# A hybrid decoder step on one core: four value pages per TensorE round, causal pooling as banded products, page suffix sums under the input GEMM

## The chip, the cores and the metric

The kernel runs on one core of a Trainium2 chip. The metric is the device time of one execution in microseconds (us). The profile shows the five engines: TensorE (PE, with PEld for its weight loads), VectorE (DVE), ScalarE (ACT), GpSimd (POOL) and SyncE (SP), whose queue issues most DMA transfers.

## The reference, cut to what matters

The program is one step of a two-layer decoder, for a prompt of 1024 tokens and for 8 decode samples with 2048 past positions each. All of it is computed; the change touches only the mixer of layer 0, which has two parts.

```
# A) forgetting attention, 8 heads x 64
logf = log_sigmoid(fl + b_forget)
# prompt: sc = q.k * scale + c_i - c_j, causal softmax, p @ v
# sample: keys and values gathered by page_table, 16 pages of 128 positions
lf_all = concatenate([lf_pool[page_table], logf_new]);  c = cumsum(lf_all)
sc = q.k_all * scale + c[past:] - c          # sum of the later log f
p  = softmax(sc);  out = p @ v_all
# B) causal pooling, 4 groups of 128 channels, windows w = 2, 4, 8, 16
dlt = (sum of the last w positions) / min(pos + 1, w) - u
y   = (dlt @ w_pool[g]) * pool_scale
```

The outputs of A and B side by side go through one output projection. Then come memory cross-attention, a SwiGLU and the whole of layer 1, all unchanged.

## The kernel before

Activations lie transposed, with 128 channels on the partitions and the 1024 prompt tokens and 8 sample tokens (`TOK` = 1032) along the free axis. A weight tile of a GEMM is split by ACT (`split_hi`) and DVE (`split_lo`, L296) into two parts, and PE takes three products per tile (`product_tile`, L311). Every engine has its own program, written out by hand, and they meet at semaphores; the order of the calls in an engine's program is the order of its work.

**The input GEMM** (`pe_ab_in`, `act_ab_in`, `dve_ab_in`, `sp_ab_in`) makes q, k, v and the pooling input u in pairs of tiles: `ab_q`, `ab_kv`, `ab_u`. Under it runs the first part of the sample attention. SP loads key pages in 64 steps of two pages (`kpage`, four slots); POOL multiplies a step by the query (`pool_keys`, L1038); DVE sums it over the head (`dve_keys`, L1044) and counts up `pages_used`, which frees the slot. 43 of the 64 steps are called for under the GEMM.

**Naturals** (`pe_naturals` and its kin) turn k and v into rows for the outputs; 8 more key steps are done beside them. ACT then issues the load of the rows `cb` that hold the prompt's cumulative gates.

**Pooling** (`dve_pool`, `pe_pool`, `act_pool`): for each of four groups DVE builds the window sums by doubling (1, 2, 3 and 4 adds of about 1023 columns, with small copies, L860 and L861), corrects the first 16 positions, subtracts u (L864 to L869), and then does 3 or 4 of the last 13 key steps. PE multiplies each group by `w_pool` (L882), ACT scales it (L889).

**Attention** (`pe_attention`, `act_attention`, `dve_attention`) is a loop of `n` over 66 turns for 8 heads times 8 query blocks. In turn n PE does the scores of block n+1 (L926), the transposes of n-1 (L971) and the values of n-2 (L988); DVE shifts the scores and takes the maximum (L943, L945), then normalizes block n-1 (L963); ACT takes the exponential (L956) and copies. The size of a block is i+1 units of 128 keys, with i = n mod 8. The sample attention lies in the same loop:

- in turn 0 the page suffix sums: products with a triangular and an all-ones matrix (L1054, L1055) and 15 chained adds over later pages (L1071 to L1074);
- in turn 1 the sample softmax, a chain over DVE, POOL, DVE, ACT, DVE, POOL, DVE (L1083 to L1094);
- from turn 2 on one step of two value pages in each turn (`pe_sample_values`, L1119): two products of a 128 x 8 stationary operand with 128 x 512 values into PSUM partitions 0 to 7. After 8 steps one sample is done and its rows are masked with `own` (L1128), summed by head (L1133) and copied (L1138).

POOL builds `own` and the causal masks `cbd` (L916) after its last key step. SP loads the value pages (L1027) four steps ahead and, in step 32, x (L1031).

## Time and profile before

| what | us |
|---|---|
| median of 3 runs | 4024.74 |
| runs | 4025.58, 4024.74, 4014.41 |
| the profiled execution | 4027.45 |
| its span, first to last instruction | 4025.7 |
| PE busy (share of the span) | 3559.6 (88%) |
| DVE busy | 1495.4 (37%) |
| mean granted PE clock | 0.942 |
| input GEMM to its last tile | up to 239 |
| naturals, pooling | 239 to 268, 268 to 323 |
| attention of layer 0 | 323 to 682 |

Read it by stage: a share of the whole span says nothing of the stage that the change touches. Positions below are us from the first instruction. PE's matrix products are pipelined, so the start-to-start distance is what one of them costs, and the duration shown includes the way through the array.

### The profile page before, as it was taken

The numbers are of one execution on the slowest core, as the hardware profiler recorded it, in microseconds if no ns is written. First come the engines' busy times: TensorE is split into PE (matmuls) and PEld (weight loads), VectorE is DVE, ScalarE is ACT, GpSimd is POOL, SyncE is SP. The second block draws the span as 40 slices with busy tenths as digits, with TensorE's granted clock in tenths as the row PEclk, the third lists the DMA queues.
The fourth block names the chain that finished last, engine by engine and source line by source line (L and its number), as shares of the span: only waits on it lengthen the run. The fifth ranks groups of instructions, "written<-read, shape, count | busy, mean of one in ns | idle before, by whom it ended". The sixth has DMA issues, their size and how long they took to land.

```text
span 4025.7 us, 54253 instructions
## 1 busy us (share of the span) xinstructions
PE 3559.6 (88%) x21068; PEld 3225.3 (80%) x21068; DVE 1495.4 (37%) x2162; ACT 1005.0 (25%) x1326; POOL 525.5 (13%) x239
## 2 busy tenths in 40 slices
PE   7966999889979999999889986768899799999996
PEld 6952445879679999999778975657897799999996
DVE  1575333443353212212522448754342521221225
ACT  2112333242222101111322323433332311111112
POOL 0771000210030000000310014002101300000003
PEclk9977999999989999999899998889999899999997
DMA  3772342134311111111022112331352011111111
GB/s 128 222 236 84 119 160 84 42 115 138 109 37 42 42 47 47 42 47 42 26 79 67 47 39 96 125 121 49 103 173 79 26 47 47 47 42 47 47 35 54
DMA packets 366668, 319.73 MB, mean 79 GB/s; under 512 B 19616, under 2 KB 308817, under 8 KB 366147
## 3 DMA queue, kind: packets, MB, share of 16 engines
q1 hardware_dynamic: 354783, 299.86, 24.3%
q10 hardware_dynamic: 11620, 17.77, 1.2%
q8 instruction: 72, 1.18, 0.1%
q0 software_dynamic: 144, 0.52, 0.0%
q14 instruction: 49, 0.40, 0.0%
HBM read 287.69 MB, written 30.74 MB: 79 GB/s over the span
## 4 chain that ended last, share of the span: by engine, by line
PE 78%; DVE 10%; issue 4%; DMA 3%; ACT 3%; POOL 1%; SPq 0%; DVEq 0%; ACTq 0%; POOLq 0%
PE ps L311 62%; PE ps L1119 3%; PE ps L926 2%; PE ps L988 2%; PE ps L1543 1%; PE ps L1565 1%; PE ps L971 1%; DVE spl_w L296 1%; DVE x L1338 1%; PE ps L681 1%; DMA acc<-spill_d 1%; DMA raw_w<-in_w_xv 1%; PE ps L1521 1%; ACT x L1352 1%; DVE acc L2160 1%
## 5 line engine op out<-in xcount | busy, mean ns | idle before, releaser
L311 PE MATMUL ps<-xs,spl_w 128*128 128x344 f32 x12528 | 2007.6, 323 | 52.9 <-DVE spl_w L296 24.8
L311 PEld LDWEIGHTS ps<-xs,spl_w 128*128 128x128 f32 x12528 | 2001.1, 190 | 57.1 <-issue 27.2
L296 DVE TENSOR_TENSOR spl_w<-raw_w,spl_w 128x1024 fp32r<-128x1024 f32 x268 | 338.4, 1263 | 757.8 <-ACT spl_w L292 753.6
L311 PE MATMUL ps<-hs,spl_w 128*128 128x344 f32 x3168 | 512.6, 325 | 27.5 <-DVE hs L1756 27.5
L311 PEld LDWEIGHTS ps<-hs,spl_w 128*128 128x128 f32 x3168 | 511.1, 192 | 29.1 <-issue 29.1
L292 ACT CAST spl_w<-raw_w 128x1024 fp32r<-128x1024 f32 x268 | 279.6, 1043 | 390.2 <-PE ps L311 362.6
L1292 POOL MEMSET sum_x<- 128x1032 f32 x6 | 5.9, 984 | 1661.2 <-DVE hs L1756 1373.8
L1754 DVE TENSOR_TENSOR sum_x<-sq,ps 128x1032 f32<-128x1032 f32 x44 | 54.0, 1228 | 351.4 <-PE ps L311 351.4
L1300 POOL TENSOR_TENSOR sum_x<-sum_x,x 128x1032 f32<-128x1032 f32 x48 | 116.1, 2418 | 474.3 <-DVE x L1260 188.1
L1038 POOL TENSOR_TENSOR kpage<-kpage,qb 128x1024 f32<-128x1024 f32 x64 | 163.2, 2577 | 101.6 <-DMA kpage<-in_cache_fox_k 101.6
L1344 POOL TENSOR_TENSOR x<-x,sum_x 128x1032 f32 x48 | 138.6, 2895 | 199.9 <-DVE x L1338 199.9
L1738 ACT CAST hs<-sum_x 128x1032 f32 (+1 forms) x44 | 46.4, 1054 | 472.0 <-DVE sum_x L1754 472.0
L1260 DVE SCALAR_TENSOR_TENSOR x<-x,ps 128x1032 f32 (+1 forms) x48 | 58.9, 1228 | 267.0 <-PE ps L311 267.0
L1278 ACT ACTIVATE sq<-x 128x1032 f32 (+1 forms) x48 | 51.2, 1067 | 420.4 <-DVE x L1260 233.5
L1269 DVE TENSOR_TENSOR sum_sq<-sum_sq,sq 128x1032 f32<-128x1032 f32 x48 | 107.6, 2241 | 92.2 <-ACT sq L1278 60.3
L1262 DVE TENSOR_TENSOR x<-x,ps 128x1032 f32 (+1 forms) x40 | 49.2, 1229 | 242.5 <-PE ps L311 242.5
L326 PE MATMUL ps<-xs,spl_w 128*128 128x344 f32 x432 | 78.7, 341 | 62.2 <-DVE xs L1356 62.2
L1119 PE MATMUL ps<-vpage,lf_pg 128*8 128x512 f32 x256 | 130.3, 634 | 2.4 <-DVE s_sum L1138 2.4
L311 PE MATMUL ps<-mem_s,spl_w 128*128 128x256 f32 x768 | 101.9, 291 | 33.9 <-DVE spl_w L296 18.3
L1734 ACT ACTIVATE sq<-ps 128x1032 f32<-128x1032 f32 x44 | 45.5, 1033 | 339.7 <-PE ps L311 336.1
L311 PEld LDWEIGHTS ps<-mem_s,spl_w 128*128 128x128 f32 x768 | 96.2, 196 | 40.7 <-DVE spl_w L296 21.2
L326 PEld LDWEIGHTS ps<-xs,spl_w 128*128 128x128 f32 x432 | 73.6, 203 | 68.0 <-issue 47.2
(350 smaller groups left out, 3064.6 us busy)
## 6 DMA issues: line engine op xcount, KB each, us to landing
kpage<-in_cache_fox_k SPq DMA_DIRECT2D x128, 256.0 KB, 3.3
vpage<-in_cache_fox_v SPq DMA_DIRECT2D x128, 256.0 KB, 2.8
raw_w<-in_w_gate SPq DMA_DIRECT2D x44, 512.0 KB, 3.8
...
```

What stands on the lines that cost most here:

```text
L292: act.copy(spl_w[:, s, 0], raw_w[:, s]).then_inc(hi_ready, 1)
L296: dve.tensor_tensor(spl_w[:, s, 1], raw_w[:, s], spl_w[:, s, 0].bitcast(F32), ALU.subtract).then_inc(lo_ready, 1)
L311: mm = pe.matmul(ps[:, 3 * s + t, 0:width], spl_w[:, s, a, k], part[:, k, width * t:width * (t + 1)], start=(k == 0 and step == 0), stop=( ...
L326: mm = pe.matmul(ps_set[s][:, t], spl_w[:, s, a, k], act_in[:, b, k, TB * t:TB * (t + 1)], start=(k == 0 and step == 0), stop=(k == DC - 1 ...
L926: mm = pe.matmul(score_ps[n % 2][:, k0:k1], proj[r, h // 2, P * i:P * (i + 1)], proj[r, 4 + h // 2, k0:k1], start=True, stop=True)
L988: mm = pe.matmul(ps[head_rows(h), 6, 0:P], proj[:, 8 + h // 2, v0:v0 + FD], pT[:, n % 2, j], start=(j == 0), stop=(j == i))
L1038: pool.tensor_tensor(kpage[:, slot], kpage[:, slot], qb[:, b % 2].unsqueeze(1).to_broadcast([P, 2, FW]), ALU.mult).then_inc(sem("keys_mult ...
L1119: mm = pe.matmul(ps[0:FH, 7, :], s_prob[:, b, :, g], vpage[:, slot, e], start=(g == 0), stop=(g == NPG - 1))
L1260: ins = dve.scalar_tensor_tensor(out=xm, in0=xm, scalar=ALPHA, in1=ps_set[s], op0=ALU.mult, op1=ALU.add)
L1269: dve.tensor_tensor(sum_sq[:], sum_sq[:], sq[:], ALU.add).then_inc(sem("sq_used"), 1)
L1300: pool.tensor_tensor(sum_x[:], sum_x[:], chunk(x, 2 * i + s), ALU.add).then_inc(sem("sum_x_ready"), 1)
L1344: pool.tensor_tensor(xk, xk, sum_x[:], ALU.add).then_inc(sem("ln_shifted"), 1)
```

## The change

It does three things.

**Pooling.** The window mean minus the token is linear in the tokens, so it becomes a product with a banded 128 x 128 matrix. POOL builds four of them (`band`, with 16-column pieces `edge` for the first tokens and for the block before) by memsets and selects, `pool_bands`, ahead of its first key step. PE first multiplies u by `w_pool`, with the tokens on the output partitions (`mapped`), ACT copies that to SBUF (`u_nat`), PE multiplies by the band (`averaged`), ACT scales. The samples go apart, in four small products. DVE's window adds are gone; the 13 last key steps move into the attention turns 0 to 6, two to a turn.

**Page suffix sums.** They leave turn 0. Products and copies go into the input GEMM between its pairs of tiles, the chained adds into DVE's program in the first `ab_u` tile; the sum with the new token's gate goes into the sample softmax, which moves to turn 7.

**Value pages.** Four pages form a round. Their products write PSUM partitions 0 to 31, 32 to 63, 64 to 95 and 96 to 127, each with a 128 x 32 stationary operand (4 samples by 8 heads). 32 rounds in turns 8 to 65 take the place of 64 steps. `own` is now 128 partitions high (spread by one product) and `sel_row` picks the sample's rows. At the head of the value loads SP now waits for the 13 stores that it waited for in step 32.

```diff
-            pe_stream(pe, "ab_kv", xs, part=(1, 4))
-            pe.wait_ge(dve_steps, step("lf_turned"))
+            pe_stream(pe, "ab_kv", xs, part=(1, 2))
+            pe_suffix(pe, 0)
+            pe_suffix(pe, 1)
+            pe_stream(pe, "ab_kv", xs, part=(2, 3))
+            pe_suffix(pe, 2)
+            pe_suffix(pe, 3)
+            pe_stream(pe, "ab_kv", xs, part=(3, 4))
+            pe.wait_ge(sem("suffix_copied"), 8)
...
+                    if g in (G0["ab_kv"] + 2, G0["ab_kv"] + 3) and s == 0:
+                        for q in range(2):
+                            dve_suffix(dve, 2 * (g - G0["ab_kv"] - 2) + q)
+                    if g == G0["ab_u"] and s == 0:
+                        dve_later_pages(dve)
...
         def dve_pool(dve):
...
             dve.wait_ge(sem("state_taken"), 4)
             dve.wait_ge(set_free[1], G1["ab_u"])
             dve.wait_ge(set_free[0], G1["ab_u"])
...
+            us = proj[:, 12:16, SEQ:TOK]
+            chain(dve, "dve")(dve.tensor_tensor(dlt_s[:], st_sum[:], us, ALU.add))
             for g, w in enumerate(WINDOWS):
...
+                dve.scalar_tensor_tensor(out=dlt_s[:, g], in0=dlt_s[:, g], scalar=1.0 / w, in1=us[:, g],
                                          op0=ALU.mult, op1=ALU.subtract).then_inc(sem("pool_ready"), 1)
...
+
+        u_ps = [ps[:, 0:2, :].rearrange("p a n -> p (a n)"), ps[:, 2:4, :].rearrange("p a n -> p (a n)")]
+        y_ps = [ps[:, 4:6, :].rearrange("p a n -> p (a n)"), ps[:, 6:8, :].rearrange("p a n -> p (a n)")]
         def pe_pool(pe):
             pe.wait_ge(set_free[0], G1["ab_u"])
             pe.wait_ge(act_steps, step("s_nat_ready"))
...
+            pe.wait_ge(act_steps, step("ulast_ready"))
+            pe.wait_ge(sem("v_copied"), NT)
+            pe.wait_ge(pool_steps, step("band3"))
+
+            def mapped(g):
+                if g >= 2:
+                    pe.wait_ge(act_steps, step(f"u_nat{g - 2}"))
+                for i in range(NT):
+                    mm = pe.matmul(u_ps[g % 2][:, P * i:P * (i + 1)], proj[:, 12 + g, P * i:P * (i + 1)], w_pl[:, g],
+                                   start=True, stop=True)
+                mm.then_inc(pe_steps, mark(f"u_mapped{g}"))
+
+            def averaged(g):
+                pe.wait_ge(act_steps, step(f"u_nat{g}"))
                 if g >= 2:
                     pe.wait_ge(sem("pool_copied"), g - 1)
...
+                y = y_ps[g % 2]
+                for i in range(NT):
+                    t0 = P * i
+                    if i == 0:
+                        pe.matmul(y[:, 16:P], u_nat[:, g, 0], band[:, g, 16:P], start=True, stop=True)
+                        pe.matmul(y[:, 0:16], u_nat[:, g, 0], edge[:, 0, g], start=True, stop=True)
+                    else:
+                        pe.matmul(y[:, t0:t0 + P], u_nat[:, g, i], band[:, g], start=True, stop=False)
+                        mm = pe.matmul(y[:, t0:t0 + 16], u_nat[:, g, i - 1], edge[:, 1, g], start=False, stop=True)
                 mm.then_inc(sem("pool_products"), 1)
+            mapped(0)
+            for g in range(4):
+                if g < 3:
+                    mapped(g + 1)
+                averaged(g)
+            pe.wait_ge(sem("pool_ready"), 4)
+            pe.wait_ge(act_steps, step("u_nat3"))
+            for g in range(4):
+                mm = pe.matmul(ps[:, 0, DECB * g:DECB * (g + 1)], w_pl[:, g], dlt_s[:, g], start=True, stop=True)
+            mm.then_inc(sem("pool_products"), 1)
+
         def act_pool(act):
+            def nat(g):
+                act.wait_ge(pe_steps, step(f"u_mapped{g}"))
+                act.copy(u_nat[:, g].rearrange("p i n -> p (i n)"), u_ps[g % 2]).then_inc(act_steps, mark(f"u_nat{g}"))
+            nat(0)
             for g in range(4):
+                if g < 3:
+                    nat(g + 1)
                 act.wait_ge(sem("pool_products"), g + 1)
...
+                act.activation(proj[:, 12 + g, 0:SEQ], y_ps[g % 2], ACT.Copy,
                                scale=col("pool_scale", g)).then_inc(sem("pool_copied"), 1)
+            act.wait_ge(sem("pool_products"), 5)
+            for g in range(4):
+                ins = act.activation(proj[:, 12 + g, SEQ:TOK], ps[:, 0, DECB * g:DECB * (g + 1)], ACT.Copy,
+                                     scale=col("pool_scale", g))
+            ins.then_inc(sem("pool_copied"), 1)
...
-        KEYS_POOL = KEYS_AB + NT
-        VALUES_FROM = 2
+        KEYS_ATT = KEYS_AB + NT
+        SOFTMAX_AT = 7
+        VALUES_FROM = 8
+        N_GROUP = N_STEP // 2
+        def keys_beside(n):
+            return range(KEYS_ATT + 2 * n, min(KEYS_ATT + 2 * n + 2, N_STEP))
+        def value_group(n):
+            return next((m for m in range(N_GROUP) if VALUES_FROM + m * (N_ATT + 1 - VALUES_FROM) // (N_GROUP - 1) == n), None)
         def sample_done(n):
-            u = n - VALUES_FROM
-            return u // (NPG // 2) - 1 if u > 0 and u % (NPG // 2) == 0 else None
+            m = value_group(n)
+            return m // 4 - 1 if m and m % 4 == 0 else None
...
+            sp.wait_ge(sem("stored"), 16 * 13)
             for u in range(N_STEP):
                 sp.wait_ge(pages_used, N_STEP + u - 3)
...
         def pe_suffix(pe, q):
-            if q:
-                pe.wait_ge(sem("suffix_copied"), 2 * q)
+            if q == 0:
+                pe.wait_ge(dve_steps, step("lf_turned"))
+            if q >= 2:
+                pe.wait_ge(sem("suffix_copied"), 2 * (q - 1))
             src = lf_flat[:, 256 * q:256 * (q + 1)]
-            pe.matmul(ps[:, 7, 0:256], later[:], src, start=True, stop=True)
-            pe.matmul(ps[:, 7, 256:512], ones[:], src, start=True, stop=True).then_inc(sem("suffix_ready"), 1)
+            pe.matmul(ps[:, 6 + q % 2, 0:256], later[:], src, start=True, stop=True)
+            pe.matmul(ps[:, 6 + q % 2, 256:512], ones[:], src, start=True, stop=True).then_inc(sem("suffix_ready"), 1)
...
         def pe_sample_values(pe, u):
-            b, slot = u // (NPG // 2), u % 4
-            pe.wait_ge(page_loaded[slot], 32 * ((N_STEP + u) // 4 + 1))
+            b = u // (NPG // 2)
+            for v in (u, u + 1):
+                pe.wait_ge(page_loaded[v % 4], 32 * ((N_STEP + v) // 4 + 1))
             if u == 0:
+                pe.wait_ge(act_steps, step("own_ready"))
                 pe.wait_ge(dve_steps, step("sc_ready"))
                 pe.wait_ge(sem("suffix_copied"), 8)
             if u % (NPG // 2) == 0 and b:
                 pe.wait_ge(sem("s_own_step"), 2 * b)
-            for e in range(2):
-                g = 2 * (u % (NPG // 2)) + e
-                mm = pe.matmul(ps[0:FH, 7, :], s_prob[:, b, :, g], vpage[:, slot, e], start=(g == 0), stop=(g == NPG - 1))
-            mm.then_inc(pages_used, 1)
+            for j in range(4):
+                g = 2 * (u % (NPG // 2)) + j
+                mm = pe.matmul(ps[32 * j:32 * (j + 1), 7, :], s_prob[:, 4 * (b // 4):4 * (b // 4 + 1), :, g],
+                               vpage[:, (u + j // 2) % 4, j % 2], start=(g < 4), stop=(g >= NPG - 4))
+                if j % 2:
+                    mm.then_inc(pages_used, 1)
         def dve_sample_own(dve, b):
             if b == 0:
-                dve.wait_ge(pool_steps, step("own_ready"))
+                dve.wait_ge(act_steps, step("own_ready"))
             dve.wait_ge(pages_used, N_STEP + (NPG // 2) * (b + 1))
             if b >= 2:
                 dve.wait_ge(sem("s_columns"), b - 1)
-            dve.tensor_tensor(s_own[:, b % 2], ps[0:FH, 7, :], own, ALU.mult).then_inc(sem("s_own_step"), 1)
+            dve.tensor_tensor(s_own[:, b % 2], ps[:, 7, :], own, ALU.mult).then_inc(sem("s_own_step"), 1)
         def pe_sample_columns(pe, b):
             pe.wait_ge(sem("s_own_step"), 2 * b + 1)
             for c in range(4):
-                mm = pe.matmul(ps[:, 7, c:c + 1], s_own[:, b % 2, P * c:P * (c + 1)], ones[0:FH, 0:1], start=True, stop=True)
+                mm = pe.matmul(ps[:, 7, c:c + 1], s_own[:, b % 2, P * c:P * (c + 1)], sel_row[:, b % 4:b % 4 + 1], start=True, stop=True)
             mm.then_inc(sem("s_columns"), 1)
...
+        def pool_bands(pool):
+            then = chain(pool, "pool")
+            pool.wait_ge(dve_steps, step("inv_cnt_ready"))
+            pool.wait_ge(sem("x_back"), 16)
+            pool.wait_ge(sem("xs_lo"), DC)
+            for g, w in enumerate(WINDOWS):
+                d, first, prev = band[:, g], edge[:, 0, g], edge[:, 1, g]
+                pool.memset(d, 1.0 / w)
+                then(pool.memset(prev, 1.0 / w))
+                pool.affine_select(out=first, in_=inv_cnt[:, g], compare_op=ALU.is_ge, fill=0.0, base=0,
+                                   pattern=[[1, 16]], channel_multiplier=-1)
+                pool.affine_select(out=prev, in_=prev, compare_op=ALU.is_ge, fill=0.0, base=w - 1 - P,
+                                   pattern=[[-1, 16]], channel_multiplier=1)
+                then(pool.affine_select(out=d, in_=d, compare_op=ALU.is_ge, fill=0.0, base=0,
+                                        pattern=[[1, P]], channel_multiplier=-1))
+                then(pool.affine_select(out=first, in_=first, compare_op=ALU.is_ge, fill=0.0, base=w - 1,
+                                        pattern=[[-1, 16]], channel_multiplier=1))
+                then(pool.affine_select(out=d, in_=d, compare_op=ALU.is_ge, fill=0.0, base=w - 1,
+                                        pattern=[[-1, P]], channel_multiplier=1))
+                then(pool.tensor_tensor(first, first, ident[:, 0:16], ALU.subtract))
+                pool.tensor_tensor(d, d, ident[:], ALU.subtract).then_inc(pool_steps, mark(f"band{g}"))
...
         def pool_attention(pool):
             for u in range(N_STEP):
                 pool_keys(pool, u)
+                if u == KEYS_ATT - 1:
+                    pool_mask(pool, 0)
             pool_own(pool)
-            pool_mask(pool, 0)
             pool_mask(pool, 1)
             pool_sample_softmax(pool)
...
-                if n == 0:
-                    for q in range(4):
-                        pe_suffix(pe, q)
                 if sample_done(n) is not None:
                     pe_sample_columns(pe, sample_done(n))
-                if n >= VALUES_FROM:
-                    pe_sample_values(pe, n - VALUES_FROM)
+                if n == SOFTMAX_AT:
+                    pe_own(pe)
+                if value_group(n) is not None:
+                    pe_sample_values(pe, 2 * value_group(n))
...
-                if n == 1:
+                if n == SOFTMAX_AT:
+                    act_own(act)
...
-                if n == 0:
-                    for q in range(4):
-                        dve_suffix(dve, q)
-                    dve_later_pages(dve)
-                if n == 1:
+                for u in keys_beside(n):
+                    dve_keys(dve, u)
+                if n == SOFTMAX_AT:
                     dve_sample_softmax(dve)
```

How the programs move, at three places. First PE in the attention loop, before (turns 3 and 4; L926 scores, L971 transposes, L988 values, L1119 value pages):

```order
L926 MATMUL ps<-proj 128x512 [waits scores_shifted]
L926 MATMUL ps<-proj 128x128
L971 MATMUL ps<-ident,prob 128x128 [waits pT_copied,prob_ready]
L971 MATMUL ps<-ident,prob 128x128 x2
L988 MATMUL ps<-pT,proj 64x128 [waits out_copied,pT_copied]
L988 MATMUL ps<-pT,proj 64x128
L1119 MATMUL ps<-vpage,lf_pg 8x512 [waits page_loaded1]
L1119 MATMUL ps<-vpage,lf_pg 8x512
```

And in the changed kernel (turns 8 to 10; L966 scores, L1011 transposes, L1028 values, L1169 value pages):

```order
L1169 MATMUL ps<-vpage,lf_pg 32x512 [waits dve_steps,act_steps,suffix_copied,page_loaded1,page_loaded0]
L1169 MATMUL ps<-vpage,lf_pg 32x512 x3
L966 MATMUL ps<-proj 128x384 [waits scores_shifted]
L1011 MATMUL ps<-ident,prob 128x128 [waits pT_copied,prob_ready]
L1028 MATMUL ps<-pT,proj 64x128 [waits out_copied,pT_copied]
L1028 MATMUL ps<-pT,proj 64x128 x7
L1169 MATMUL ps<-vpage,lf_pg 32x512 [waits page_loaded3,page_loaded2]
L1169 MATMUL ps<-vpage,lf_pg 32x512 x3
L966 MATMUL ps<-proj 128x512 [waits scores_shifted]
L1011 MATMUL ps<-ident,prob 128x128 [waits pT_copied,prob_ready]
L1011 MATMUL ps<-ident,prob 128x128
L1028 MATMUL ps<-pT,proj 64x128 [waits out_copied,pT_copied]
```

Two products in each turn become four in about every second turn, with no wait between the four. Second DVE in the input GEMM of the changed kernel, from the end of the gate sums to the second tile of the first `ab_u` pair (L304 splits a weight tile, L1093 sums a key step):

```order
L781 TENSOR_TENSOR gates<-gates 128x8 [waits dve_chain] x6
L782 TENSOR_TENSOR gates<-gates 128x8x7 [waits dve_chain]
L304 TENSOR_TENSOR spl_w<-raw_w,spl_w 128x1024 [waits hi_ready]
L1118 TENSOR_TENSOR lf_pg<-lf_pg 128x8x8 [waits suffix_copied]
L1118 TENSOR_TENSOR lf_pg<-lf_pg 128x8x8 [waits dve_chain] x14
L1120 TENSOR_TENSOR suf<-suf,lf_pg 128x8x120 [waits dve_chain]
L1093 TENSOR_REDUCE sc<-kpage 128x2x8 [waits keys_multiplied,dve_chain]
L1093 TENSOR_REDUCE sc<-kpage 128x2x8 [waits keys_multiplied] x3
L304 TENSOR_TENSOR spl_w<-raw_w,spl_w 128x1024 [waits hi_ready]
```

The 16 sums (L1118, L1120) now stand ahead of four key steps and of the next tile's split. Third DVE at the start of attention in the changed kernel (L872 and L874 prepare the samples' pooling, L1316 is the first instruction of attention, L985 and L983 shift scores):

```order
L872 TENSOR_TENSOR dlt_s<-st_sum,proj 128x32 [waits set0_free,set1_free,state_taken]
L874 SCALAR_TENSOR_TENSOR dlt_s<-dlt_s,proj 128x8 [waits dve_chain]
L874 SCALAR_TENSOR_TENSOR dlt_s<-dlt_s,proj 128x8 x3
L1316 MEMSET sc 128x64 [waits pool_copied]
L985 ISA prob,tmax<-ps,cbd 128x128 [waits masked,scores_ready,dve_steps]
L985 ISA tmax 128x1
L988 TENSOR_REDUCE nmax<-tmax 128x1 [waits scores_shifted]
L1093 TENSOR_REDUCE sc<-kpage 128x2x8 [waits keys_multiplied] x2
L983 ISA prob,tmax<-ps,cb 128x128 [waits scores_ready]
```

Between the samples' pooling and the first scores DVE does no key step any more; the first two come in turn 0.

## Rows read from the trace of the kernel before

**Rows 1.** The page: busy time of the engines.
```profile
PE 3559.6 (88%) x21068; PEld 3225.3 (80%) x21068; DVE 1495.4 (37%) x2162; ACT 1005.0 (25%) x1326; POOL 525.5 (13%) x239
```

**Rows 2.** Windows: stretch and length, busy us (instructions) by engine, granted clock, DMA.
```profile
100.00:239.00 139.00, 137.79 (x879) 137.70 (x879) 81.90 (x71) 26.26 (x29) 108.58 (x44) 1.00 0.75 228
268.00:323.00 55.00, 14.90 (x24) 7.39 (x24) 54.48 (x55) 3.76 (x4) 32.55 (x12) 0.53 0.43 130
323.00:358.80 35.80, 13.43 (x29) 6.47 (x29) 20.79 (x59) 5.56 (x11) 7.59 (x7) 0.54 0.17 52
390.70:679.20 288.50, 286.06 (x1225) 133.14 (x1224) 92.94 (x382) 96.73 (x224) 11.74 (x5) 0.97 0.39 124
```

**Rows 3.** Timeline, PE and ACT in attention: start us, us, engine line, shapes.
```profile
390.70 1.89 PE L1119 MATMUL ps<-vpage,lf_pg 128*8 128x512 f32 x4
...
444.03 1.89 PE L1119 MATMUL ps<-vpage,lf_pg 128*8 128x512 f32 x4
...
445.85 1.55 PE L926 MATMUL ps<-proj 64*128 64x512 f32 x4
...
457.68 0.88 PE L971 MATMUL ps<-ident,prob 128*128 128x128 f32 x6
```

**Rows 4.** Source lines L1119 and L1565: ns min/median/max of one, first and last start.
```profile
L1119 PE MATMUL ps<-vpage,lf_pg x256: 589/592/1061, 358.8 to 678.7; 128*8 128x512 f32 x128
L1565 PE MATMUL ps<-mkv,smz x128: 592/592/617, 1038.7 to 3059.2; 128*32 128x512 f32 x128
```

**Rows 5.** Timeline: DVE after the naturals and in pooling, last scaling on ACT.
```profile
267.61 2.04 DVE L828 TENSOR_TENSOR s_qk<-s_nat 8x512 f32<-8x512 f32 x1 [2.24 <-ACT s_nat L811]
...
293.36 2.19 DVE L860 COPY win<-win 128x4 f32<-128x4 f32 x1
...
298.81 0.16 DVE L865 TENSOR_TENSOR win<-win,inv_cnt 128x16 f32<-128x16 f32 x1
...
322.61 1.12 ACT L889 ACTIVATE proj<-ps,cols 128x1032 f32<-128x1032 f32 x1 [15.48 <-PE ps L882]
```

**Rows 6.** Timeline: short products with 128-column weights; the issue of the loads of cb.
```profile
477.88 1.05 PE L1133 MATMUL ps<-ones,s_own 8*128 8x1 f32 x8
...
270.70 0.83 ACTq L910 DMA_DIRECT2D cb<-c_d  x2
```

**Rows 7.** Timeline, the start of attention.
```profile
324.69 0.70 PE L1054 MATMUL ps<-lf_pg,later 128*128 128x256 f32 x2
...
328.13 0.29 DVE L945 CUSTOM_DVE_ANT_0 prob<-ps,cbd 128x128 f32<-128x128 f32 x1 [4.18 <-POOL cbd L916]
...
338.13 3.85 DVE L1071 TENSOR_TENSOR lf_pg<-lf_pg 128x64 f32<-128x64 f32 x15
343.21 1.23 DVE L1074 TENSOR_TENSOR kst<-kst,lf_new 128x1024 f32<-128x1024 f32 x1
...
345.48 2.01 DVE L1083 TENSOR_TENSOR sc<-sc,kst 128x1024 f32<-128x1024 f32 x1
...
356.27 0.41 DVE L943 CUSTOM_DVE_ANT_0 prob<-ps,cb 128x256 f32<-128x256 f32 x1
...
358.84 3.58 PE L1119 MATMUL ps<-vpage,lf_pg 128*8 128x512 f32 x4
```

**Rows 8.** Timeline and source line: the chain of one key step.
```profile
276.56 3.46 DVE L1044 TENSOR_REDUCE sc<-kpage 128x16 f32<-128x1024 f32 x3
...
282.61 2.34 POOL L1038 TENSOR_TENSOR kpage<-kpage,qb 128x1024 f32<-128x1024 f32 x1 [7.49 <-DMA kpage<-in_cache_fox_k]
...
L1038 POOL TENSOR_TENSOR kpage<-kpage,qb x64: 2338/2403/3430, 114.1 to 315.1; 128x1024 f32<-128x1024 f32 x64
```

**Rows 9.** The chain of waits: one pair of tiles of the GEMM (start us, us).
```profile
101.86 22.72 PE ps L311 x144
```

**Rows 10.** DMA of x and of value pages: KB each, median us to landing.
```profile
vpage<-in_cache_fox_v SPq DMA_DIRECT2D x35, 256.0 KB, 2.9
x<-x_d SPq DMA_DIRECT2D x1, 4128.0 KB, 13.6
```

115 lines of the change are left out of this document (53 added, 62 removed).

## The prediction

> **What bounds the kernel now.** I read the page first, for the share of each engine: PE is busy 88% of the span [rows 1]. That says only where to look, so I cut layer 0's mixer into windows [rows 2]. In the input GEMM PE is busy 137.8 of 139 us at full clock: whatever is put on PE there is paid in full. In pooling PE is busy 14.9 of 55 us and DVE 54.5: DVE bounds. In the first 35.8 us of attention PE is busy 13.4 us, held by the suffix sums and the sample softmax. From turn 8 to the end, 288.5 us, PE is busy 286.1 and DVE only 92.9: there PE is the bound, and DVE, ACT and DMA have room. Last I read single places in the timeline, to see what an instruction costs there.
>
> All of this lies on the path: the output projection can start only when the last sample is done. So time gained in a stage is gained at the end, if the next stage does not wait for something else.
>
> **The sum, part by part.**
>
> *GEMM.* The suffix products are eight matrix products of 256 columns, each two instructions on PE. The first four of them took 0.70 us for two with the tail [rows 7]; from the value pages, 512 columns cost 0.43 us (below), so 256 cost about 0.21: 16 x 0.21 = 3.4 us, on a full PE. With the seams between tiles: +4. The 16 sums on DVE took 3.85 us for the 15 [rows 7] while POOL had no key page, plus some 1.2. Here POOL multiplies nearly all the time (108.6 of 139 us [rows 2]), and a DVE instruction can be held by it: a copy of 4 columns took 2.19 us, a similar operation 0.16 [rows 5]. But DVE, busy with the sums, frees no key slot, so POOL has at most four steps to hold it with, 2.4 us each [rows 8]: the sums take 7 to 14 us, once. A tile lasts 11.4 us on PE (half of the 22.72 of a pair [rows 9]), and the next tile's split is not needed until it ends, so I cost PE at nothing; if that cover fails, up to 5 us. The key steps slip by some 3 us, which is hidden by the +4. The copies (eight of 0.4 us) are hidden likewise. SP and POOL issue nothing new there; `pool_bands`, 36 small instructions, stands before the first key step at 114 us [rows 8], where POOL waits for the first key page anyway: nothing.
>
> The Trainium skill (SBUF — State Buffer, "Who interferes with whom") says that the pair of ports shared by DVE and GpSimd is an exclusive lock for a whole instruction. The 2.19 us row agrees. If each of the 16 sums met a multiplication, they would take 16 x 2.4 = 38 us, and PE would wait some 22 of them: the forecast would be that much later.
>
> *Pooling.* It began when the naturals ended, 267.6 [rows 5], now 271.6. DVE's adds go. PE has per group 8 products with `w_pool` and 16 with the bands, two instructions each; with the samples' it is 200 instructions. Instructions of 128 columns go at about 0.12 us (six transposes in 0.88, tail included [rows 3]), and even one-column ones with 128-column weights at 0.12 (eight in 1.05 [rows 6]), since the weight load does not shrink: 200 x 0.12 = 24 us. The clock in this stretch was 0.53 [rows 2], that is mostly the 1.2 GHz level; the first instructions will go at half speed: +4. ACT cannot start its copies before it has issued the loads of `cb` (270.7 [rows 6], now some 4 later), which overlaps the first products. At the end come the last scaling (1.12 us [rows 5]) and the samples' four: 2.5. Pooling ends at 302; before, with that last scaling, at 323.7 [rows 5]. ACT has 2.2 us of work per group against PE's 6, so it is hidden.
>
> *Turns 0 to 8.* The first scores no longer wait for the mask, which POOL now builds in the pooling stage; before, DVE shifted only at 328.1 [rows 7]. The suffix work is gone. In its place DVE does 13 key steps. Four are multiplied by then; the others wait for slots. A freed slot took 5 us until POOL could start on it again (DVE's sums begin at 276.56 and take 1.2 us each, POOL starts at 282.61 [rows 8]), then 2.4 us of POOL for each step. So step 55 is ready 10.7 us after the start, step 63 after 10.7 + 8 x 2.5 = 31, and DVE reaches the softmax at 34. The products of turns 0 to 6 are shorter and lie beside this. The softmax took 345.48 to 356.27 = 10.8 us, now with one add more (1.23, the moved L1074): 12; then 2.6 us to the first value page (358.84 [rows 7]), and 1 for the longer block of this turn. The first round falls at 302 + 50 = 352; before, turn 8 reached its value pages at 390.7 [rows 3]. Savings up to here: 39 us.
>
> *Turns 8 to 65.* A step of two pages costs PE 1.82 us (L1119 at 444.03, the next L926 at 445.85 [rows 3]): four instructions, 0.43 apart and 0.1 of change, though each one lasts 0.59 [rows 4]. 58 steps lie in this stretch: 105.6 of the 288.5 us, the rest is 183. Now there are 32 rounds of eight instructions. The 32 columns of weights cost nothing extra: L1565, with 128 x 32 weights, lasts the same 0.592 as L1119 [rows 4]. What a round costs depends on whether products in different column groups of the array run beside each other, and **no row shows that**: all column-narrow products of this kernel follow others in the same columns. Bounds: one after the other, 8 x 0.43 + 0.1 = 3.5 us; all four beside each other, 2 x 0.43 + 0.15 = 1.0. I take the middle. Each product is two instructions for the same columns, which must follow each other, and the program gives them in order (first and second of page 0, first and second of page 1, ...). If starts keep that order, the second of one page can run beside the first of the next, and no more: 5 slots of 0.43, plus a little for each change: 2.4 us. 32 x 2.4 = 77. With less work on PE, DVE's chain of shift, normalize, transpose shows in the shortest blocks: +3. So 183 + 77 + 3 = 263 in place of 288.5: another 25 saved. Value pages are not the limit: 1 MB per round in 8 us, landing in 2.9 us for 256 KB, and x took 13.6 us [rows 10] where two rounds of pages are in stock.
>
> Sum: 39 + 25 = 64 us against the profiled 4027.45, or 3963; the profiled execution lies 2.7 above the median, so against the median of 4024.74 I say **3960**.
>
> **The rivals.**
>
> *A. Four column groups truly at once*, a round costs 1.0: 32 us in place of 77, 45 less: 3915. For it: the work of a round fits the array, and the code puts no wait between the four. Against: the order within each pair of instructions. The Trainium skill (TensorE: Matmul & The Clock Gate, "Packing small matmuls") gives 2.38 times for three column tiles of 512 columns. By that a round would be 3.5 / 2.38 = 1.5 us, an estimate, and the forecast 29 lower.
>
> *B. No overlap between column groups*, a round costs 3.5: 112 us, 35 more: 3995. The gain is then that of pooling and suffix sums, and the number of PE instructions for the values is the same as before. For it: every row of PE shows one instruction after the other.
>
> *C. Slower than before: PE's clock.* Turns 8 to 65 ran at 0.97; the stretches in which PE was half idle at 0.53 and 0.54 [rows 2]. If the changed loop leaves PE so many gaps that the clock falls to 1.2 GHz, the some 260 us of it double at most: 4220 if throughout. It outweighs the gain of 64 once about a quarter of the stretch runs at the lower level. Against: rounds and blocks still keep PE over 90% busy after turn 8.
>
> *D. The change gains at fewer places than it says:* the key steps, now in turns 0 to 6, and the moved sums come 10 to 25 us later than worked out (locks between POOL and DVE): 3970 to 3985, with a round as in the forecast.
>
> **How the numbers follow.** My forecast 0.45, A 0.17, B 0.23, C 0.04, D 0.11. The likeliest gives 3960. The range holds the forecast, A, B and D with some us for the stages around: 3903 to 4003; outside lie C and the ends of A and B. About 0.3% (12 us) is what a measurement can tell: faster 0.94 (all but C and an adding up of B and D), same 0.03, slower 0.03.
>
> **What would show it.** In the changed trace: the GEMM ends 4 us later with no gap at L319 in the `ab_u` tiles; the first scores follow at about 302; PE over 85% busy there after ACT's first copy; the key steps L1093 paced by POOL in turns 2 to 6; the softmax ending near 348 and the first L1169 near 352. Decisive is the distance from a round's first L1169 to the next L966: 2.4 us by my reading, 1.0 by A, 3.5 by B. I am wrong if that distance is 3.5 or 1, if the clock in turns 8 to 65 is under 0.9, or if after the softmax PE waits for DVE, ACT or a value page in most turns.

## The result, and the profile after

The changed kernel takes **3923.58 us** (median; 3921.89 to 3924.45), the kernel before 4019.89 in the same comparison (4014.41 to 4025.58): ratio 0.976, 95% interval 0.9741 to 0.9778. I had said 3960 with a range of 3903 to 4003. The sign and the range hold; the time is 36 us below the likeliest value. The range holds it because it was drawn wide enough for rival A, which I had given a chance of 0.17. By the two profiled executions the gain is 105.5 us (spans 4025.7 and 3920.2), more than the 96.3 of the medians, since the profiled execution of before was slower than its other runs. The stages are compared by these two traces.

The page of the changed kernel, the row that answers to [rows 1]:

```profile
PE 3491.0 (89%) x21246; PEld 3237.0 (83%) x21246; DVE 1475.7 (38%) x2129; ACT 1010.8 (26%) x1335; POOL 528.2 (13%) x275
```

PE has 178 instructions more and is busy 68.6 us less: the first sign that instructions overlap on PE itself.

Windows of the changed kernel (stretch, length, busy us and instructions of PE, PEld, DVE, ACT and POOL, granted clock, DMA share, GB/s): input GEMM, naturals, pooling, turns 0 to 8, turn 8 to the last value round. They answer to [rows 2].

```profile
100.00:247.60 147.60, 143.65 (x898) 142.50 (x897) 92.48 (x93) 26.27 (x30) 102.80 (x42) 0.99 0.67 209
247.60:279.50 31.90, 16.91 (x84) 12.68 (x84) 18.15 (x23) 7.86 (x12) 22.73 (x10) 0.63 0.97 321
279.50:302.90 23.40, 22.54 (x200) 22.47 (x200) 1.85 (x7) 9.01 (x12) 11.60 (x5) 0.99 0.27 74
302.90:360.00 57.10, 40.57 (x124) 23.78 (x124) 46.66 (x87) 17.10 (x36) 27.75 (x16) 0.56 0.45 134
360.00:578.20 218.20, 209.74 (x1249) 124.30 (x1248) 97.64 (x382) 96.99 (x224) 12.78 (x6) 0.98 0.56 177
```

| stage | before | after | moved by | I had said |
| --- | --- | --- | --- | --- |
| input GEMM (from 100) | 139.2 | 147.6 | +8.4 | +4 |
| naturals | 28.4 | 31.9 | +3.5 | 0 |
| pooling | 56.1 | 23.4 | -32.7 | -26 |
| scores 0 to first values of turn 8 | 67.0 | 57.1 | -9.9 | -17 |
| turns 8 to 65 | 288.5 | 218.2 | -70.3 | -25.5 |

Together -101; some 4.5 us more differ behind this stretch, where the code is the same.

The decisive distance, from the first value product of a round to the next block's scores (timeline, PE and its weight loads; start us, us), and the source line with ns minimum, median and maximum of one:

```profile
393.13 0.23 PEld L1169 LDWEIGHTS ps<-vpage,lf_pg 128*32 128x32 f32 x8 [0.17 <-issue]
393.13 1.10 PE L1169 MATMUL ps<-vpage,lf_pg 128*32 128x512 f32 x8
...
394.16 0.29 PEld L966 LDWEIGHTS ps<-proj 64*128 64x128 f32 x2 [0.80 <-issue]
```
```profile
L1169 PE MATMUL ps<-vpage,lf_pg x256: 592/614/1070, 360.0 to 577.6; 128*32 128x512 f32 x128
```

A round of eight instructions takes 1.03 us. One of them still takes 0.6, as before [rows 4], and all eight weight loads are through in 0.23 us. That is my rival A. The distance of 1 is also one of the signs by which I had said that I would be wrong.

One round falls out of line. The value page issued behind the load of `x` lands late, PE waits for it, and the clock falls (timeline of PE, then its window; last a window of the kernel before, behind the end of a sample):

```profile
471.28 1.94 PE L1169 MATMUL ps<-vpage,lf_pg 128*32 128x512 f32 x8 [4.07 <-DMA vpage<-in_cache_fox_v]
473.15 3.78 PE L966 MATMUL ps<-proj 64*128 64x512 f32 x4
```
```profile
471.20:479.80 8.60, 8.52 (x25) 4.02 (x26) 2.22 (x7) 0.80 (x1) 0.00 (x0) 0.50 0.59 198
```
```profile
479.30:483.30 4.00, 4.00 (x6) 0.88 (x7) 1.42 (x7) 0.82 (x2) 0.00 (x0) 0.57 0.27 67
```

After 4.07 us of waiting PE works for 8.6 us at 0.50, the lower level of 1.2 GHz: this round takes 1.87 us and the scores behind it 3.78. So the late page costs 4.1 us of waiting and, at half speed, some 4.3 more (an estimate, half of 8.6). The kernel before has five stretches of about 4 us like the one shown, each behind the end of a sample (from 479, 520, 561, 602 and 643), where PE did eight one-column products and waited 0.35 us. Together they are worth some 8.5 us (an estimate, from their clocks). The changed kernel has the same products and waits there and none of these stretches; why is open.

Where the input GEMM lost its time (timeline; first DVE, then POOL, then PE):

```profile
204.22 8.12 DVE L1118 TENSOR_TENSOR lf_pg<-lf_pg 128x64 f32<-128x64 f32 x15
...
213.57 4.60 DVE L1093 TENSOR_REDUCE sc<-kpage 128x16 f32<-128x1024 f32 x4
...
232.14 2.23 DVE L304 TENSOR_TENSOR spl_w<-raw_w,spl_w 128x1024 fp32r<-128x1024 f32 x1
```
```profile
219.58 2.39 POOL L1087 TENSOR_TENSOR kpage<-kpage,qb 128x1024 f32<-128x1024 f32 x1 [10.68 <-DMA kpage<-in_cache_fox_k]
```
```profile
234.42 1.80 PE L319 MATMUL ps<-xs,spl_w 128*128 128x344 f32 x5 [2.70 <-DVE spl_w L304]
```

The sums fit under a tile, as I had said. But the four key steps behind them free their slots only from 213.57 on, POOL stands 10.7 us without a page, the next four key steps wait for POOL, and the split of the next weights, which DVE's program puts behind them, ends at 234.4. PE waits for it.

The stretch up to the softmax (timeline, DVE, then PE):

```profile
310.92 2.10 DVE L1003 TENSOR_SCALAR prob<-prob,rinv 128x256 f32<-128x256 f32 x1
...
335.08 3.13 DVE L1003 TENSOR_SCALAR prob<-prob,rinv 128x768 f32<-128x768 f32 x1
...
338.14 1.21 DVE L1093 TENSOR_REDUCE sc<-kpage 128x16 f32<-128x1024 f32 x1
...
340.86 0.69 DVE L1003 TENSOR_SCALAR prob<-prob,rinv 128x896 f32<-128x896 f32 x1
341.46 2.02 DVE L1128 TENSOR_TENSOR sc<-sc,suf 128x1024 f32<-128x1024 f32 x1
...
359.99 1.25 PE L1169 MATMUL ps<-vpage,lf_pg 128*32 128x512 f32 x8
```

DVE reaches the softmax 38.5 us after the first scores, not 34. Normalizes of 256 and of 768 columns took 2.10 and 3.13 us beside work on POOL (a multiplication, and the building of the next mask); one of 896 columns without it took 0.69. In this stretch DVE waited for POOL's key steps only once, 1.7 us; otherwise it was busy itself, and PE ran at the lower level of its clock (window of the changed kernel):

```profile
302.90:341.40 38.50, 29.68 (x73) 15.61 (x74) 35.22 (x66) 11.33 (x26) 25.11 (x13) 0.50 0.58 173
```

### The profile page after: what moved, and what is told of

It is laid out like the page before. It is cut to its first block, busy times and chain, and to the rows that moved or that the text cites. A ratio compares the mean times of both kernels' runs of the same rounds, so it can differ in the third digit from the quotient of the medians.

```text
span 3920.2 us, 54635 instructions
## 1 busy us (share of the span) xinstructions
PE 3491.0 (89%) x21246; PEld 3237.0 (83%) x21246; DVE 1475.7 (38%) x2129; ACT 1010.8 (26%) x1335; POOL 528.2 (13%) x275
## 4 chain that ended last, share of the span: by engine, by line
PE 76%; DVE 10%; DMA 4%; issue 4%; ACT 3%; POOL 2%; SPq 1%; DVEq 0%; ACTq 0%; POOLq 0%
PE ps L319 63%; PE ps L1028 2%; PE ps L966 2%; PE ps L1628 1%; PE ps L1650 1%; DVE spl_w L304 1%; PE ps L1011 1%; DMA raw_w<-in_w_xv 1%; DVE acc L2245 1%; PE ps L1169 1%; DVE x L1423 1%; POOL kpage L1087 1%; PE ps L705 1%; DMA acc<-spill_d 1%; PE ps L1606 1%
## 5 line engine op out<-in xcount | busy, mean ns | idle before, releaser
L304 DVE TENSOR_TENSOR spl_w<-raw_w,spl_w 128x1024 fp32r<-128x1024 f32 x268 | 339.7, 1267 | 759.5 <-ACT spl_w L300 754.9
L1423 DVE TENSOR_TENSOR x<-x,sum_sq 128x1032 f32 (+1 forms) x48 | 105.0, 2201 | 0.0
```

The lines of the kernel that those rows point to most:

```text
L304: dve.tensor_tensor(spl_w[:, s, 1], raw_w[:, s], spl_w[:, s, 0].bitcast(F32), ALU.subtract).then_inc(lo_ready, 1)
L1423: dve.tensor_tensor(xk, xk, sum_sq[:], ALU.mult).then_inc(sem("ln_scaled"), 1)
```

## Experiments

Two questions were open. What makes a round cheap, and how far do the products of different column groups get past each other? And what is the move of the suffix sums worth, with the key steps behind it? Eleven runs answer them, each beside its own runs of the kernel before. Executions of one kernel scattered by up to 18.5 us in the runs of the second question, so that there a place in the trace decides and the median only supports it.

### One column group

```diff
-                mm = pe.matmul(ps[32 * j:32 * (j + 1), 7, :], s_prob[:, 4 * (b // 4):4 * (b // 4 + 1), :, g],
-                               vpage[:, (u + j // 2) % 4, j % 2], start=(g < 4), stop=(g >= NPG - 4))
+                mm = pe.matmul(ps[0:32, 7, :], s_prob[:, 4 * (b // 4):4 * (b // 4 + 1), :, g],
+                               vpage[:, (u + j // 2) % 4, j % 2], start=(g == 0), stop=(g == NPG - 1))
```

(and the heads' own rows taken from 32 partitions in place of 128.)

> The changed kernel with all four value products of a round in the same column group (output partitions 0 to 31), so that nothing can run beside something else; as many instructions, bytes and turns as before. Theory (most of the saving beyond the pooling stage comes from four column groups at once; a round now costs 1.03 us on PE): a round costs 8 x 0.43 + 0.1 = 3.5 us, 32 rounds 2.5 us each more, the time is 3924 + 79 = 4003. Rival (the saving comes from fewer and denser steps, the number of groups does not matter): 3924 to 3935.

Measured: 3992.85 us (3990.3 to 3994.93), ratio to before 0.9916 (0.99 to 0.9933). Timeline and window of this kernel:

```profile
441.18 3.65 PE L1169 MATMUL ps<-vpage,lf_pg 128*32 128x512 f32 x8
444.75 0.91 PE L966 MATMUL ps<-proj 64*128 64x384 f32 x2
```
```profile
360.00:649.50 289.50, 286.11 (x1247) 146.24 (x1245) 94.02 (x383) 96.09 (x221) 12.14 (x5) 1.00 0.44 133
```

A round takes 3.57 us, and the stretch 289.5, about what the kernel before took with 58 steps of 1.82 (288.5); its first round began at 358.8, 1.2 us ahead of the window. So four groups are worth 71 us in this stretch, 69 by the medians, and everything else that the change does 33 (before took 4026.02 beside this run). By rounds it would be 32 x 2.54 = 81, and the expectation, 4003, was built on that; 10 us are given back. With short rounds PE is idle 8.5 us of the stretch (218.20 less 209.74), with long ones 3.4, mostly because the page behind `x` comes 4.1 us late in the one and 0.5 in the other. The half speed behind that wait, the 4.3 us from above, is missing here too: the clock is 1.00.

### Two column groups, in two orders

```diff
-                mm = pe.matmul(ps[32 * j:32 * (j + 1), 7, :], s_prob[:, 4 * (b // 4):4 * (b // 4 + 1), :, g],
-                               vpage[:, (u + j // 2) % 4, j % 2], start=(g < 4), stop=(g >= NPG - 4))
+                r = j % 2
+                mm = pe.matmul(ps[32 * r:32 * (r + 1), 7, :], s_prob[:, 4 * (b // 4):4 * (b // 4 + 1), :, g],
+                               vpage[:, (u + j // 2) % 4, j % 2], start=(g < 2), stop=(g >= NPG - 2))
```

The second kernel has `r = j // 2`, with start and stop at the first and last page of each group. In both the heads' own rows are taken from 64 partitions.

> The same with two column groups, given to the four products in the order 0, 1, 0, 1. Theory (products of different groups run beside each other, the two instructions of a pair hold nobody up): two products after each other in each group, 4 x 0.43 + 0.1 = 1.8 us a round, 3924 + 32 x 0.8 = 3949. Rival (starts keep the order of the program, my reading in the prediction): slots A1, A2 with B1, B2 with A1', A2' with B1', B2' = 5 x 0.43, 2.25 us a round, 3963.

> The same with two column groups in the order 0, 0, 1, 1. Theory (each group has its own queue, deep enough for four instructions): 1.8 us a round, 3949 as with 0, 1, 0, 1. Rival 1 (an instruction that must wait for its group holds up all behind it): seven slots of 0.43, 3.1 us a round, 3924 + 32 x 2.1 = 3991. Rival 2 (it is looked a few instructions ahead): between.

Measured: 3944.71 us (3941.5 to 3946.83) in the order 0, 1, 0, 1, and 3942.45 (3938.64 to 3948.06) in the order 0, 0, 1, 1. A round of the first kernel, then one of the second:

```profile
440.14 1.95 PE L1170 MATMUL ps<-vpage,lf_pg 128*32 128x512 f32 x8
442.02 1.77 PE L966 MATMUL ps<-proj 64*128 64x512 f32 x4
```
```profile
440.15 1.95 PE L1170 MATMUL ps<-vpage,lf_pg 128*32 128x512 f32 x8
442.02 1.77 PE L966 MATMUL ps<-proj 64*128 64x512 f32 x4
```

Both take 1.88 us a round: four slots of 0.43 and a little. With one group it was eight slots, with four groups it is two. My reading, in which the second instruction of a pair holds up what is behind it, asks for five slots in the first order; it falls. So does rival 1 of the second run, the waiting instruction that blocks the line, with its seven slots in the second order: the trace has the eight starts of this round in twos, at 440.15 and 440.16, 440.63 and .64, 441.06 and .07, 441.49 and .50. What counts is the work that each group gets; every kernel here loads its groups evenly, so what an uneven load costs is not shown. At least four instructions for one group can stand ahead of those of another without holding them up; a longer run was not tried. The Trainium skill (TensorE: Matmul & The Clock Gate, "Packing small matmuls") says that matmuls are "pc-monotone in start AND end — strict FIFO, no reordering". By that the second order would cost the seven slots; the 1.88 us speak against it for products in different column groups, and the measurement decides.

### Eight columns of weights in place of 32

```diff
-                mm = pe.matmul(ps[32 * j:32 * (j + 1), 7, :], s_prob[:, 4 * (b // 4):4 * (b // 4 + 1), :, g],
+                mm = pe.matmul(ps[32 * j:32 * j + FH, 7, :], s_prob[:, b, :, g],
```

(and the sample's columns taken with the first column of `sel_row`.)

> The changed kernel with weights of 8 columns (the one sample) in place of 32 (four samples) for each group, in the same four groups of the array. Theory (a product costs by the 512 columns of values that pass, not by its weights' columns): a round stays at 1.03 us, 3924 within 5. Rival (weight loads count, now that products run beside each other): 32 x 0.1 to 0.3 less, 3914 to 3921.

Measured: 3923.81 us (3920.98 to 3930.53). A round:

```profile
446.16 1.05 PE L1169 MATMUL ps<-vpage,lf_pg 128*8 128x512 f32 x8
447.15 0.70 PE L966 MATMUL ps<-proj 64*128 64x256 f32 x2
```

It takes 0.99 us, 0.04 less, which is 1.3 us over 32 rounds and not to be seen in the time. The 32 columns are free within that, as the prediction said.

### The sums in the pooling stage

```diff
-                    if g == G0["ab_u"] and s == 0:
-                        dve_later_pages(dve)
...
                                          op0=ALU.mult, op1=ALU.subtract).then_inc(sem("pool_ready"), 1)
+            dve_later_pages(dve)
```

> The changed kernel with the 15 sums over the pages and the add behind them moved on DVE from the first tile of the last input GEMM to the pooling stage, where DVE has 21.7 us of nothing. Theory (the 8.1 us of sums make the next split of weights late, which costs PE two gaps of together 5.7 us and a slow start behind them): the input GEMM ends at 240 to 243 in place of 247.6, the pooling stage keeps its 23.4 us, and the time is 3915 to 3919. Rival (the split is late because POOL's key steps are, whatever DVE sums): GEMM end 246 or later, time 3921 to 3926.

Measured: 3919.68 us (3915.97 to 3920.58), all five executions below the lowest of the changed kernel. PE at the end of its GEMM, and the start of pooling:

```profile
224.81 18.47 PE L319 MATMUL ps<-xs,spl_w 128*128 128x344 f32 x116
...
273.95 3.81 PE L890 MATMUL ps<-w_pl,proj 128*128 128x128 f32 x32 [1.56 <-issue]
```

PE runs through the seam without a gap, the GEMM ends at 243.3, which leaves the +4 of the suffix products alone, and pooling starts at 273.95 in place of 279.60. The expectation counted one gap twice: the 5.7 us were 2.7 of PE and 3.0 of its weight loads, the same wait. The rest of the 4.3 us by which the GEMM ends earlier is the clock: in the changed kernel the 4 us behind the gap, 234.4 to 238.4, ran at 0.61, worth 1.6 us, and here nothing of the GEMM from 219 us on runs below full clock. The output projection begins at 578.2 in place of 584.1.

### The suffix work back in turn 0

In `pe_attention`, then in `dve_attention` behind the first shift; both are taken out of the input GEMM, and the products use bank 7 alone again:

```diff
+                if n == 0:
+                    for q in range(4):
+                        pe_suffix(pe, q)
...
+                if n == 0:
+                    for q in range(4):
+                        dve_suffix(dve, q)
+                    dve_later_pages(dve)
```

> The changed kernel with the suffix products, their copies and the page sums put back into turn 0 of attention, the rest as changed. Theory (moving them is worth what they took there, less what they cost in the input GEMM): GEMM ends at 239 to 240, 8 earlier; turn 0 longer by the four products with copies (4 x 1.5) and 4 to 8 of sums, of which the key chain behind it hides little: time 3921 to 3929, so that this part of the change is worth under 5 us. Rival (as the prediction priced it, GEMM +4 against some 12 in attention): 3931 or more.

Measured: 3931.67 us (3925.77 to 3939.74). The GEMM ends at 239.6, pooling starts 9.5 us earlier than in the changed kernel, and the stretch from first scores to values, which ends with the first value page at 365.1, is 71.6 us in place of 57.1 (the window shown runs 0.9 us further):

```profile
293.50:366.00 72.50, 47.94 (x146) 27.54 (x146) 50.65 (x111) 18.22 (x43) 28.12 (x16) 0.58 0.35 106
```

By medians moving the suffix work is worth 8 us, the rival's number; the profiled execution, the fastest of the five, is only 3.9 above that of the changed kernel. By place, the output projection begins at 590.9 in place of 584.1, 6.8 later; behind that the same code took 2.9 us less in this execution. So it is worth 4 to 8, and the run does not settle more: of the 14.5 us that the stretch behind the first scores saves, 9.5 are paid ahead of pooling.

### Key steps in the pooling stage

```diff
+            for v in range(KEYS_AB + NT, KEYS_ATT):
+                dve_keys(dve, v)
...
-        KEYS_ATT = KEYS_AB + NT
+        KEYS_ATT = KEYS_AB + NT + 8
```

The loop stands at the end of `dve_pool`; the mask stays behind step 50 on POOL.

> The changed kernel with key steps 51 to 58 on DVE in the pooling stage, and five left for the first turns of attention. Theory (the stretch from the first scores to the first value page, 57.1 us, is set by the chain of key steps on DVE and POOL up to the sample softmax): steps done 15 to 20 us earlier, softmax still at turn 7 so that turns 0 to 7 are bounded by attention itself, 57 falls to 42 to 47, time 3909 to 3914. Rival (DVE's long normalizes, held by POOL, and PE's half clock set it): 52 to 57, time 3919 to 3924.

Measured: 3926.79 us (3921.28 to 3931.64): nothing gained. DVE, POOL and PE of this kernel:

```profile
292.64 1.22 DVE L1095 TENSOR_REDUCE sc<-kpage 128x16 f32<-128x1024 f32 x1 [9.83 <-POOL kpage L1089]
...
329.69 0.82 DVE L985 CUSTOM_DVE_ANT_0 prob<-ps,cb 128x640 f32<-128x640 f32 x1 [3.30 <-PE ps L968]
...
342.75 2.04 DVE L1130 TENSOR_TENSOR sc<-sc,suf 128x1024 f32<-128x1024 f32 x1
```
```profile
287.95 2.35 POOL L958 TENSOR_TENSOR cbd<-cb,future 128x1024 f32<-128x1024 f32 x1 [10.97 <-DMA cb<-c_d]
290.26 30.04 POOL L1089 TENSOR_TENSOR kpage<-kpage,qb 128x1024 f32<-128x1024 f32 x13
```
```profile
325.00:342.70 17.70, 17.70 (x60) 10.34 (x60) 7.25 (x28) 6.22 (x14) 0.00 (x0) 0.62 0.08 27
```

Two things came out. POOL's mask stands ahead of key step 51 and waits 11 us for the row of `cb`, so the steps came late in pooling and the first scores with them (DVE's shift at 310.2). And with the key steps done by 321.6, DVE still reached the softmax at 342.75 (changed kernel: 341.46), because PE, at clock 0.62 (0.5 is the lower level, 1.2 GHz) and busy without a break, was the bound of turns 4 to 6. The stretch up to turn 8 has two bounds close together, the key chain and PE near its lower level. Taking away one shows the other. By place this execution even lost: its output projection begins at 591.7, 7.6 later than in the changed kernel, and only 1.3 of that stand ahead of the first value page. A good part of the rest is PE at the lower clock: 11.3 us in place of 8.6 behind the late page, and 7 us more, from 389.5, at 0.51 behind a wait of 1.1 us for DVE.

Then both moves together, with an earlier softmax:

```diff
-                    if g == G0["ab_u"] and s == 0:
-                        dve_later_pages(dve)
...
+            dve_later_pages(dve)
+            for v in range(KEYS_AB + NT, KEYS_ATT):
+                dve_keys(dve, v)
...
-        SOFTMAX_AT = 7
-        VALUES_FROM = 8
+        SOFTMAX_AT = 4
+        VALUES_FROM = 5
```

> Both moves together, and the sample softmax at turn 4 in place of 7 with the value pages from turn 5. Theory: the gains of the two add up (6 + 12), and the rounds fill gaps of PE in turns 5 to 8: 3900 to 3908, below both kernels. Rival (sums and key steps collide in the pooling stage, the key chain then ends as late as before and turn 4 waits for it): 3912 to 3922.

Measured: 3915.09 us (3911.95 to 3922.48), ratio to before 0.973 (0.9712 to 0.9748). DVE and PE of this kernel:

```profile
304.80 0.29 DVE L986 CUSTOM_DVE_ANT_0 prob<-ps,cbd 128x128 f32<-128x128 f32 x1
...
320.90 2.01 DVE L1129 TENSOR_TENSOR sc<-sc,suf 128x1024 f32<-128x1024 f32 x1
```
```profile
339.55 1.23 PE L1170 MATMUL ps<-vpage,lf_pg 128*32 128x512 f32 x8
...
456.25 1.94 PE L1170 MATMUL ps<-vpage,lf_pg 128*32 128x512 f32 x8 [7.38 <-DMA vpage<-in_cache_fox_v]
```
```profile
456.20:469.60 13.40, 13.35 (x39) 6.93 (x39) 3.84 (x14) 2.46 (x5) 0.00 (x0) 0.50 0.41 134
```

The first values fall at 339.6, 20 us earlier than in the changed kernel, and only 4.6 us of time are gained over the sums alone. Part of the rest was work that PE had to do anyway. Another part is the page behind the load of `x`: PE waited 7.4 us for it and then worked 13.4 us at 0.50, together some 14 us, where the changed kernel lost 8.4 at this place (estimates, with half of the slow stretch). No run moved the load of `x`, so what this place would give is not shown.

Two tries to let POOL start the keys earlier failed, and a third moved only rounds.

```diff
-                if u == KEYS_ATT - 1:
+                if u == 57:
                     pool_mask(pool, 0)
...
-        KEYS_ATT = KEYS_AB + NT
+        KEYS_ATT = KEYS_AB + NT + 11
```

> As with both moves, but on POOL the mask of the first head stands behind key step 57 in place of 50, DVE does 11 of the 13 steps in the pooling stage (two are left for turn 0), the softmax is in turn 2 and the values from turn 3. Theory (in the last two runs POOL sat 11 us behind the mask, which waits for the row of c, with key pages already there; so DVE waited for POOL in the pooling stage and the first scores came at 304.6 to 310): the key steps start near 271, all are done at 301 to 305, the first shift falls at 298 to 300 with pooling starting at 274.8, the sample softmax ends near 316, and the output projection starts at 560 to 570 in place of 577.6: time 3896 to 3907. Rival (turns 0 to 7 at half clock bound this stretch whatever the key chain does): the output projection at 571 or later, 3908 to 3916.

Measured: 3920.62 us (3914.92 to 3931.24). DVE did the sums before the waiting key steps, so their four slots came free from 285 on and POOL stood once more:

```profile
285.07 4.60 DVE L1094 TENSOR_REDUCE sc<-kpage 128x16 f32<-128x1024 f32 x4
...
311.27 0.29 DVE L986 CUSTOM_DVE_ANT_0 prob<-ps,cbd 128x128 f32<-128x128 f32 x1
```
```profile
291.32 7.03 POOL L1088 TENSOR_TENSOR kpage<-kpage,qb 128x1024 f32<-128x1024 f32 x3 [11.50 <-DMA kpage<-in_cache_fox_k]
```

```diff
+            for v in range(KEYS_AB + NT, KEYS_AB + NT + 4):
+                dve_keys(dve, v)
+            dve_later_pages(dve)
+            for v in range(KEYS_AB + NT + 4, KEYS_ATT):
+                dve_keys(dve, v)
```

> The changed kernel; DVE in the pooling stage: the four key steps that are multiplied by then (51 to 54), then the sums, then steps 55 to 57; the mask stands behind step 57 on POOL; six steps are left for turns 0 to 2, the softmax is in turn 3, the values from turn 4. Theory (in the run before, DVE did its sums first, freed the four key slots only at 285 to 290, and POOL stood 11.5 us without a page; the shift of the first scores came at 311): slots freed at 276 to 281, POOL on again at 281 to 284, the first shift at 298 to 300, softmax from 313 on, output projection at 568 to 573 in place of 582.8: time 3905 to 3911, less than with sums in the pooling stage alone (3920). Rival (whatever comes earlier on DVE is lost in turns 3 to 7, which PE does at its lower clock): 3913 to 3920.

Measured: 3921.23 us (3914.43 to 3932.97). Now the slots came free from 283 on, but POOL multiplied beside the sums, and these took 10.07 us, where they had taken 3.84 with the sums alone moved to this stage:

```profile
286.42 10.07 DVE L1121 TENSOR_TENSOR lf_pg<-lf_pg 128x64 f32<-128x64 f32 x15
...
303.38 0.29 DVE L988 CUSTOM_DVE_ANT_0 prob<-ps,cbd 128x128 f32<-128x128 f32 x1
```

The theories of both runs fall on their time, and both times lie above the rivals' ranges as well. By place the first begins its output projection at 582.9 (560 to 570 expected) and the second at 579.0 (568 to 573 expected), 1.2 and 5.1 us earlier than the changed kernel; behind that the same code took 3.4 us more in the second one's execution. Both have the late page too, 4.3 and 4.4 us, with nearly 14 us at clock 0.50 behind it in place of 8.6. Whether PE's clock or DVE took the rest in turns 3 to 7 they do not tell apart.

The rounds moved, in the kernel with the mask behind step 57:

```diff
-            return next((m for m in range(N_GROUP) if VALUES_FROM + m * (N_ATT + 1 - VALUES_FROM) // (N_GROUP - 1) == n), None)
+            turns = [3, 5, 7] + [NT * h + i for h in range(1, FH) for i in (0, 1, 3, 5)] + [N_ATT]
+            return turns.index(n) if n in turns else None
```

> The same, with the rounds of value pages at turns 3, 5, 7, then at blocks 0, 1, 3 and 5 of each head and at the end, in place of every other turn. Theory (with rounds of 1.03 us PE's only waits behind turn 8 are those in a head's short blocks, 1.8 us for DVE, and 4.1 for one page behind the load of x): a round in a short block fills such a gap: 1 to 4 us less than the run before. Rival (two rounds in neighbouring short blocks empty the four page slots, PE waits for pages): 3 to 10 us more.

Measured: 3917.72 us (3913.93 to 3923.93), 2.9 below its neighbour with ranges that overlap: open.

The best version is the one with sums and key steps in the pooling stage and the softmax in turn 4: 3915, below both kernels. Against the changed kernel the 8.5 us are likely and not settled, since the two intervals against before overlap.

## Why the prediction was right in sign and too small

- **Bound.** Right: DVE in pooling, PE from turn 8 on. The two large gains lie where the windows put them.
- **Round of value pages, "If starts keep that order ... 5 slots of 0.43 ... 2.4 us".** This step failed, and it is nearly the whole miss: 32 x (2.4 - 1.03) = 44 us. No row of before showed two column groups, so I chose between 1.0 and 3.5 by an order of starts that I had only argued. The two-group runs show no such order, in either arrangement. Rival A had the mechanism and its price of 1.0. That the time came out only 36 us low is in part luck: the stages ahead of turn 8 saved 8.3 us less than I had said.
- **"183 + 77 + 3".** The other two terms add up, 218.2 less 32 x 1.03 is 185 where I had 186, but by chance. The 183 read off before held some 8.5 us of PE at the lower clock, which I took for work and which the changed kernel does not have, and 2.4 of waits. Without them about 172 are left, and the run with one group has about the same: 290.7 from its first round on, less 32 x 3.57, less 3.4 of waits, is 173. In the changed kernel 8.5 of waits and 4.3 at half speed came on top. My 3 for DVE's chain stands against 1.8 us of PE waiting for normalizes; half of the rest is the 4.1 for the page behind `x`, which I had excluded by the stock of two rounds.
- **Input GEMM, "+4 ... I cost PE at nothing; if that cover fails, up to 5 us".** The products cost the 3.5 to 4 us (the run with the sums moved ends its GEMM 4.1 later than before). The cover failed, by 4.3. I had looked at how long the sums take and not at what stands between them and the next split in DVE's program: "the key steps slip by some 3 us, which is hidden" is the failing sentence. They slipped by over 9 (from 204.2, where the sums begin, to 213.6), POOL ran dry, and the split waited behind POOL. The estimate from the Trainium skill (SBUF — State Buffer, "Who interferes with whom"), 38 us of sums, did not come: they took 8.1. POOL ran out of pages at 208.9, in the middle of them, as I had argued from its four slots.
- **Naturals at no change.** They took 3.5 us more. DVE entered them with late key steps, but that is not all: with the sums moved to pooling they still took 30.7 us (243.3 to 273.95), and with no suffix work in the GEMM at all 30.5 (239.6 to 270.1), where before took 28.4. So about 1 us goes with the sums, and the cause of the other 2 is open.
- **Pooling, "200 x 0.12 = 24 ... +4 ... 2.5".** 23.4 us. The price of an instruction was right (0.113 on average); the clock supplement was not: the row at 279.50 shows 0.99. What I had read off before, 0.53, was the clock of a PE that DVE kept waiting.
- **Turns 0 to 8, 50 us.** 57. I had the key steps paced by POOL, to end after 31 us; from the seventh on DVE waited for POOL no more, and it was busy 35.2 of the 38.5 us. Normalizes held by POOL (2.10 to 3.13 us) were not in my working: 4.5 us more up to the softmax. The softmax took its 12. Behind it I had 3.6 us to the first value page and it took 6.4, with PE's transposes and values of that turn at clock 0.50: 2.9 more.
- **The rivals.** B is refuted as a mechanism; built on purpose (one group) it gives 3993, where I had said 3995, but that is two errors that cancel: its value pages of turn 8 begin 31.9 us earlier than before (358.8), not 39, and from there to the last it takes 290.7 us, not 298. C did not come as priced, 0.98 from turn 8 on; it shows in small behind the late page. D came beside A: 4.4 us over my term in the GEMM, 3.5 in the naturals, 7 in the turns.

The Trainium skill's figure (TensorE: Matmul & The Clock Gate, "Packing small matmuls") of 2.38 for three column tiles stood between my value and rival A. Here four tiles give 3.57 / 1.03 = 3.5 times and two give 3.57 / 1.88 = 1.9; three were not run.
